# Two of the middle levels of a triangular inverse: the sum formed by VectorE in SBUF instead of by TensorE in PSUM

## The reference, cut to what matters

```python
lmat = jnp.where(strict, jnp.einsum('bhtk,bhsk->bhts', kb, kh) * jnp.exp(jnp.where(strict, diff, 0.0)), 0.0)
rhs = jnp.concatenate([vh * bh[..., None], kb * jnp.exp(g)[..., None]], axis=-1)
sol = lax.linalg.triangular_solve(eye + lmat, rhs, left_side=True, lower=True, unit_diagonal=True)
v_new = u - jnp.einsum('bhtk,bhkv->bhtv', wk, S)
S_new = S * jnp.exp(gl)[..., None, None] + jnp.einsum('bhsk,bhsv->bhkv', kh * jnp.exp(gl[..., None] - g)[..., None], v_new)
```

## Time and profile before

| what | before |
|---|---|
| median of three runs | 3650.18 us |
| profiled execution, its own time | 3649.81 us |
| span of the trace | 3648.0 us |
| busy, whole span | PE 90%, PEld 82%, DVE 50%, ACT 39%, POOL 12% |
| prompt mixers | about 997 to 1713 us of the span |
| one steady tile, 1403 to 1447 us (44 us) | PE 40.3, DVE 36.8, ACT 23.0, POOL 26.0 us busy |

### The profile page before, as it was taken

One profiled execution on the slowest core, in us unless ns is written; L12 is line 12 of the kernel. 1 busy time (PEld: TensorE's weight loads), 2 busy tenths in 40 slices (PEclk: granted clock), 3 DMA queues, 4 the chain that ended last, 5 costly groups with the idle time before them and its releaser, 6 DMA issues. The chain is left out here.

```text
span 3648.0 us, 52370 instructions
## 1 busy us (share of the span) xinstructions
PE 3287.7 (90%) x21605; PEld 2988.0 (82%) x21605; DVE 1829.2 (50%) x2931; ACT 1416.9 (39%) x2100; POOL 436.4 (12%) x450
## 2 busy tenths in 40 slices
PE   5899999998289999897559979999999999999998
PEld 4899999998278888886538769999999999999987
DVE  6232333221378888885447734454454454454465
ACT  6233422322155555552025533343343343343454
POOL 0000000000156556651300000000000000000000
PEclk6899999999699999998579989999999999999999
DMA  5222233221622223221135564334444354344353
GB/s 194 50 60 67 70 72 83 83 71 57 255 76 93 96 89 98 88 75 44 39 138 214 186 234 163 133 144 153 149 173 153 118 186 150 133 146 154 133 202 116
DMA packets 232386, 450.24 MB, mean 123 GB/s; under 512 B 41383, under 2 KB 115293, under 8 KB 228029
## 3 DMA queue, kind: packets, MB, share of 16 engines
q1 hardware_dynamic: 230020, 428.33, 34.9%
q10 hardware_dynamic: 2128, 18.56, 1.4%
HBM read 363.38 MB, written 83.47 MB: 122 GB/s over the span
## 5 line engine op out<-in xcount | busy, mean ns | idle before, releaser
L2769 PE MATMUL ff_p<-ff_h_hi,ff_w_hi 128*128 128x384 f32 (+1 forms) x1536 | 502.6, 327 | 23.4 <-DMA ff_h_lo<-tmp_h 23.4
L2771 PE MATMUL ff_p<-ff_h_hi,ff_w_lo 128*128 128x384 f32 (+1 forms) x1536 | 502.8, 327 | 0.0
L2770 PE MATMUL ff_p<-ff_h_lo,ff_w_hi 128*128 128x384 f32 (+1 forms) x1536 | 501.9, 327 | 0.0
L412 PE MATMUL pin_pz<-hi,pin_whi 128*128 128x424 f32 (+1 forms) x1320 | 469.4, 356 | 14.2 <-DVE pin_wlo L528 14.2
L413 PE MATMUL pin_pz<-lo,pin_whi 128*128 128x424 f32 (+1 forms) x1320 | 467.2, 354 | 0.0
L414 PE MATMUL pin_pz<-hi,pin_wlo 128*128 128x424 f32 (+1 forms) x1320 | 467.0, 354 | 0.0
L2788 PE MATMUL ff_p<-ff_w_lo,ff_f_hi 128*128 128x512 f32 (+1 forms) x1088 | 426.7, 392 | 0.0
L2789 PE MATMUL ff_p<-ff_w_hi,ff_f_lo 128*128 128x512 f32 (+1 forms) x1088 | 426.4, 392 | 0.0
L2787 PE MATMUL ff_p<-ff_w_hi,ff_f_hi 128*128 128x512 f32 (+1 forms) x1088 | 423.8, 389 | 0.0
L2872 DVE TENSOR_TENSOR ff_w_lo<-ff_w,ff_w_hi 128x1024 fp32r<-128x1024 f32 x192 | 235.2, 1225 | 345.6 <-ACT ff_w_hi L2820 345.6
L2820 ACT ACTIVATE ff_w_hi<-ff_w 128x1024 fp32r<-128x1024 f32 x192 | 203.6, 1060 | 388.9 <-PE ff_p L2789 384.6
(11 more groups left out here) (522 smaller groups left out, 5536.5 us busy)
## 6 DMA issues: line engine op xcount, KB each, us to landing
ff_w<-in_w_unit SPq DMA_DIRECT2D x192, 512.0 KB, 5.2
ff_w<-in_w_unit SPq DMA_DIRECT2D x48, 2048.0 KB, 7.9
tmp_z<-pin_z SPq DMA_DIRECT2D x32, 1024.0 KB, 5.2
mix_rb<-tmp_rows_p SPq DMA_DIRECT2D x16, 1152.0 KB, 5.9
pin_w<-in_w_in SPq DMA_DIRECT2D x33, 512.0 KB, 8.1
gat_wa<-in_w_ada ACTq DMA_DIRECT2D x8, 2048.0 KB, 28.7
mix_zb<-tmp_z SPq DMA_DIRECT2D x16, 640.0 KB, 4.2
tmp_h<-op_h_hi SPq DMA_DIRECT2D x17, 512.0 KB, 4.1
```

Of the source, the lines that this page charges most:

```text
L412: pe.matmul(pz[:, g, 0:n], whi[:, u, k], hi[:, k, at:at + n], start=(k == 0), stop=False)
L2769: pe.matmul(dst, w1_hi[:, u, k], hi, start=(k == 0), stop=False)
L2770: pe.matmul(dst, w1_hi[:, u, k], lo, start=False, stop=False)
L2771: mm = pe.matmul(dst, w1_lo[:, u, k], hi, start=False, stop=(k == KT - 1))
```

## The change

For the levels in `ADDED`, which are 1 and 2, TensorE no longer puts X into PSUM ahead of the product: `level_update` takes the branch that levels 5 and 6 already take, six plain products with `pair_of(m1, h)`. `inverse(l)` returns at once on ScalarE. `update(l)` on VectorE first waits for the product and adds it from PSUM to `x` in place, 128 x 768, and then does what it did before for `xt`. Levels 3 and 4 keep identity and copy. All semaphores count as before.

```diff
+ADDED = (1, 2)
...
                 def level_update(l):
                     pe.wait_ge(S("xt"), v(LEVELS, l))
-                    if l < BLOCKY:
+                    if l < BLOCKY and l not in ADDED:
                         onto(update_in(l), ident_r[:, 0, :], lambda par: from_head(x, par, 4))
...
                 def inverse(l):
+                    if l in ADDED:
+                        return
                     act.wait_ge(*((S("u"), v(U, 2 * l - 1)) if l else (S("m1"), v(LEVELS, 1))))
...
                 def update(l):
+                    if l in ADDED:
+                        dve.wait_ge(S("u"), v(U, 2 * l - 1))
+                        dve.wait_ge(S("x"), v(LEVELS, l))
+                        dve.tensor_tensor(hm(x[:, 0:MH]), hm(x[:, 0:MH].bitcast(F32)), pv(update_in(l), P), ALU.add
+                                          ).then_inc(S("x"), 1)
                     if l >= BLOCKY:
```

## The result

The changed kernel takes 3690.22 us (median of six runs, 3683.09 to 3700.04), the kernel before 3650.59 (six runs, 3641.07 to 3656.53). The ratio is 1.0112, with an interval of 1.0093 to 1.0132: slower by 1.1%, where 3679 (3660 to 3712) was forecast. The profiled execution of the changed kernel is 3690.56 us with a span of 3688.8, 40.75 over that of before.

The account below looks back on a forecast made before the run. No engine's sum of work but the order of starts between TensorE, ScalarE and VectorE bounds the kernel. Delay 18.3 (tile 15's gain included) + clock 15 - collisions 4 = 29.3 on 3649.81: 3679 us, range 3660 to 3712.

Parts of the forecast that it names:

- The order of starts: Level 2: the sum for X queues behind `decays` on VectorE; level 3's product starts 2.76 us later, TensorE idle 3.96.
- The delay of a tile: Level 4's copy on ScalarE starts 1.27 us later in tiles 0 to 14, passed to the next tile: 19.1 us.
- Tile 15: The last tile, without `decays`: its sum for X at level 2 starts 0.92 earlier, takes 0.14 more, gaining 0.8 us.
- The clock: TensorE's idle ahead of level 3's product lowers its granted clock: 1.0 us a tile in 15 tiles, 15 us.
- upper bound of 1.53 a tile: Most that one slow clock stretch on TensorE costs a tile, from tile 8's copy being 1.53 us late.
- Part of the slow stretch will lie in the idle itself: Reason for pricing TensorE's slow clock at 1.0 us a tile, between bounds of 0 and 1.53.
- the clock falls in full in every tile: Rival: TensorE's slow clock costs 1.53 us in each of 15 tiles, 23 in place of 15: 3687 us; chance 0.18.
- The collisions: Scaling `y` beside GpSimd's steps, long in tiles 1 and 12: between -7.9 and 0 us, taken as -4.
- the scaling collides in most tiles: Rival: scaling `y` is held beside GpSimd in 14 tiles at 2.42 us each, 33.9: 3712 us; chance 0.12.
- Faster, by VectorE coming ahead of `mix_hk`: Rival: `mix_cc` issues before GpSimd's `mix_hk` and isn't held; 2.33 us a tile gained, 3614 us; chance 0.06.
- No difference: Rival: the 1.27 us a tile is absorbed behind level 4: 3650 us; chance 0.06.
- the clock stays up: Rival: TensorE's clock does not fall behind its idle, 18.3 - 4: 3664 us; chance 0.10.

Follow-up runs that it names:

- the third experiment: The changed kernel with level 2's sum for X written ahead of `decays` on VectorE, `xt`'s sum left behind it: 3674.88 us, ratio 0.9994 to the kernel before.
- the fourth experiment: The changed kernel with 16 unused identity matmuls in TensorE's idle ahead of level 3's product, tiles 1 to 14: 3704.99 us, ratio 1.007 to the kernel before.
- the first experiment: The changed kernel with only level 1 changed, level 2 as in the kernel before: 3683.98 us, ratio 1.0006 to the kernel before.

## Why the prediction was right, and where its size was off

*The order of starts* was right, nearly to the row. Level 2's sum for X was put 17.33 us into the tile and stands at 17.30; the product of level 3 was to be 2.76 later and is 2.74; TensorE was to stand idle 3.96 and does so 3.72. The idle is shorter mostly because level 1 gains 0.25 instead of 0.39: the sum for X starts 0.14 behind the reciprocal's end (1329.98 against 1329.84), which the prediction had at nothing. The earlier sum of the third experiment gives the loss back, and level 2 alone brings it: this cause is shown.

*The delay of a tile* was put at 1.27 and is 1.17. The copy of level 3, reckoned from tile 15, was to start 21.80 into the tile, and with the clock up starts at 21.79; that of level 4 was to start at 25.73 and starts at 25.64. With 1.30 for tile 0 (41.69 to 42.99 us) and 14 times 1.17 the term is 17.7, against 19.1.

*Tile 15* gains 0.6 instead of 0.8, by the start of its copy `mix_wn`, 35.88 into the tile before and 35.29 after.

*The clock* is the term that was mis-sized: 15 forecast, 22.8 measured. Against 44.54, the eight tiles with the shorter slow stretch are longer by 1.36 on average, together 10.9, and the five with the double one by 2.39, together 11.9. The prediction's upper bound of 1.53 a tile came from the one slow stretch in tile 8 of the kernel before; no slow stretch within the tiles 1 to 14 of that trace was longer, and five tiles went past the bound. "Part of the slow stretch will lie in the idle itself" was right in kind, but the part is small: of the 6.8 us at the lower level in tile 7, about 1.35 lie ahead of the product's start at 1339.05, and in the eight tiles with the shorter stretch at most 0.45 do. The rival "the clock falls in full in every tile" (3687) was nearer to the 3690 than the forecast. The Trainium skill's account of a wait that comes round in every pass (TensorE: Matmul & The Clock Gate, section HAM oscillation — how this bites in real kernels) agrees: 13 of the 14 steady tiles have a slow stretch at that idle. Only tile 11 has none there: it began with one, its level 2 was late, and the idle ahead of its product of level 3 was 1.99 us.

*The collisions* were put at -4 and are -3.1: before, two tiles of 3.9 over 43.37; after, one tile of 49.32 - 44.54 = 4.8. The size is right by luck, since -4 was the middle between both gone and both kept, and the reason given wasn't right. They went not because "the coincidence changes" by 1.27 us but because the slow clock moves the scaling past GpSimd's small steps; with the clock kept up, the fourth experiment has nine. The rival that the scaling collides in most tiles is thus what happens without the clock's fall.

Sum: 17.7 + 22.8 - 3.1 = 37.4, where the tiles show 37.7. The other 3.0 of the 40.75 lie outside (2.4 before tile 0, whose first step is at 999.00 against 996.63, the rest behind the first step of tile 15, net of the 0.6 that tile 15 gains); apart from that gain the change has no part there that a row shows.

*Faster, by VectorE coming ahead of `mix_hk`* did not happen, but its price was good: 2.33 a tile were reckoned, and with `mix_hk` held back a tile is 43.37 - 41.20 = 2.2 shorter. Most of it, 43.37 - 41.79 = 1.6, comes to the kernel before as well. *No difference* and *the clock stays up* are out by the tiles' lengths.

## What to carry to other kernels

Before a step is moved to another engine, look at what stands ahead of it in that engine's order at that very place: here a step of 0.95 us that replaced one of 0.81 cost 2.7 us of start, because 6 us of another job were queued ahead. An idle on TensorE in each pass has to be priced twice, as delay and as clock, and a stretch seen once is no upper bound. Two costs may also shelter each other, so an experiment that removes one should come with one that removes both, and the neighbour that does the holding is worth moving first: holding GpSimd's `mix_hk` back was worth 1.6 us a tile in the kernel before, the change on top of it 0.6.

## What the runs showed of the hardware

- Who gets in at a boundary between two GpSimd steps varies. With the scaling started 0.25 to 0.28 us before the end of the same GpSimd step, it took 1.34 us in six of the tiles 1 to 14 and 4.42 in eight, in one execution of one kernel (level 1 alone). Over executions of the kernel before it was two held tiles and one. The Trainium skill says that the one that issues first holds the shared pair for its instruction (SBUF — State Buffer, section Who interferes with whom); the 3.68 of `mix_cc` fit that, but this rule doesn't say why a waiting step is passed over by several later ones, which the rows of the first experiment show. What decides it is open: the held and the others overlap in where they start, 0.273 to 0.281 us before that end against 0.250 to 0.277.
- A step needn't have two inputs in SBUF to be held: `mix_cc` has one, takes 3.68 us beside GpSimd's `mix_hk` and 0.18 where `mix_hk` comes later.
- Around the same idle of 3.7 us TensorE spends 3.4 us at the lower clock in eight tiles and 6.8 in five. In the traces of the changed kernel (two), of level 2 alone and of the changed kernel with GpSimd's first wait, every stretch that begins by 17.92 us into the tile is of the long kind (19), and every one that begins at 17.95 or later of the short kind (35). What makes it begin earlier or later wasn't tried. A shorter idle at that place can go either way: after 1.99 us (tile 11) the clock stayed up, while in the second trace of the changed kernel two tiles with 2.02 and 2.19 us had a stretch at the lower clock.
- The same two kernels compared at 1.0112 in the result and at 1.0061 on the second chip, with intervals that don't meet, because the kernel before was slower there by 23 us and the changed one by 4. The wait that takes the collision away brought the kernel before from 3673 to 3644 there.
